# Latent attention: value products in three parts, and three PSUM banks in one rotation for turned pieces, key and query pieces and sums

## The reference

```python
def one(args):
    q_blk, i = args
    s = jnp.einsum('bhqd,bhkd->bhqk', q_blk, k).astype(jnp.float32) * scale
    s = jnp.where(kpos[None, :] <= qpos[:, None], s, neg)
    p = jax.nn.softmax(s, axis=-1).astype(v.dtype)
    return jnp.einsum('bhqk,bhkd->bhqd', p, v)
```

## Time and profile before

| What | us |
|---|---|
| median of 3 runs | 1940.0 |
| the three runs | 1933.75, 1940.00, 1941.69 |
| the profiled execution | 1935.15 |
| its span on the core | 1933.4 |
| TensorE busy | 1832.9 (95%) |
| VectorE busy | 952.6 (49%) |
| ScalarE busy | 667.7 (35%) |
| GpSimd busy | 951.8 (49%) |

### The profile page before, as it was taken

One profiled execution on the slowest core, in us unless ns is written; L12 is line 12 of the kernel. 1 busy time (PEld: TensorE's weight loads), 2 busy tenths in 40 slices (PEclk: granted clock), 3 DMA queues, 4 the chain that ended last, 5 costly groups with the idle time before them and its releaser, 6 DMA issues.

```text
span 1933.4 us, 25385 instructions
## 1 busy us (share of the span) xinstructions
PE 1832.9 (95%) x8924; PEld 1521.7 (79%) x8924; DVE 952.6 (49%) x1420; ACT 667.7 (35%) x1161; POOL 951.8 (49%) x519
## 2 busy tenths in 40 slices
PE   7999999999997888899999989889999999699998
PEld 7788888888876777778878878678888888588887
DVE  5445444000017556675245444577777777622212
ACT  7322223121014555531133222544444444422212
POOL 6733333445654776224533232677777777533230
PEclk9999999999998899999999999899999999899999
DMA  6511101453314885054222133233333333554312
GB/s 259 196 33 44 33 33 55 149 178 120 98 55 149 319 317 217 23 205 144 98 77 66 55 118 112 69 122 122 123 123 121 122 122 112 188 178 130 100 54 87
DMA packets 72667, 237.95 MB, mean 123 GB/s; under 512 B 6800, under 2 KB 17168, under 8 KB 69264
## 3 DMA queue, kind: packets, MB, share of 16 engines
q1 hardware_dynamic: 48720, 159.31, 25.0%
q10 hardware_dynamic: 23872, 77.60, 10.8%
HBM read 172.93 MB, written 63.96 MB: 123 GB/s over the span
## 4 chain that ended last, share of the span: by engine, by line
PE 64%; issue 12%; POOL 12%; DVE 6%; ACT 4%; DMA 1%; POOLq 0%; SPq 0%; ACTq 0%; DVEq 0%
PE ps L554 18%; PE ps L559 18%; PE ps L560 18%; POOL wl L483 8%; PE ps L901 3%; POOL zB L490 2%; PE ps L880 1%; ACT prow L1516 1%; PE ps L1201 1%; PE ps L1203 1%; PE ps L1202 1%; DVE p1l L1890 1%; DMA raw<-in_slabs 1%; DVE kbl L1890 0%; ACT oT L1214 0%
## 5 line engine op out<-in xcount | busy, mean ns | idle before, releaser
L451 POOL TENSOR_SCALAR wh<-raw 128x1024 fp32r<-128x1024 f32 x76 | 211.7, 2786 | 551.5 <-PE ps L554 507.9
L554 PE MATMUL ps<-uh,wh 128*128 128x512 f32 (+1 forms) x576 | 227.8, 395 | 2.4 <-issue 2.4
L560 PE MATMUL ps<-uh,wl 128*128 128x512 f32 (+1 forms) x576 | 224.8, 390 | 0.0
L559 PE MATMUL ps<-ul,wh 128*128 128x512 f32 (+1 forms) x576 | 224.4, 390 | 0.0
L453 POOL TENSOR_TENSOR wl<-raw,wh 128x1024 fp32r<-128x1024 f32 x76 | 183.0, 2408 | 6.4
L483 POOL TENSOR_TENSOR wl<-raw,wh 128x512 fp32r<-128x512 f32 x88 | 139.9, 1609 | 35.3 <-ACT wh L1214 35.3
L530 POOL TENSOR_TENSOR wl<-raw,wh 128x1024 fp32r<-128x1024 f32 x28 | 71.4, 2552 | 141.1 <-ACT wh L1214 141.1
L1893 DVE SCALAR_TENSOR_TENSOR ya<-zA,sm,ya 128x512 f32<-128x512 f32 x88 | 94.1, 1069 | 89.6 <-ACT ya L1748 81.1
L470 POOL TENSOR_TENSOR over_rings<-over_rings 128x512 f32<-128x512 f32 x88 | 112.8, 1282 | 45.9 <-DMA over_rings<-in_slabs 40.6
L1893 DVE SCALAR_TENSOR_TENSOR yb<-zB,sm,yb 128x512 f32<-128x512 f32 x88 | 127.6, 1450 | 14.4 <-ACT yb L1748 8.1
L1214 ACT ACTIVATE wh<-raw 128x512 fp32r<-128x512 f32 (+1 forms) x124 | 90.5, 749 | 114.7 <-PE ps L554 78.4
(11 more groups left out here) (434 smaller groups left out, 4842.3 us busy)
## 6 DMA issues: line engine op xcount, KB each, us to landing
raw<-in_slabs SPq DMA_DIRECT2D x134, 512.0 KB, 3.6
over_rings<-in_slabs SPq DMA_DIRECT2D x22, 1024.0 KB, 7.0
s_s<-over_rings SPq DMA_DIRECT2D x22, 1024.0 KB, 4.8
ssm<-s_s SPq DMA_DIRECT2D x22, 512.0 KB, 3.8
raw<-s_s SPq DMA_DIRECT2D x22, 512.0 KB, 4.8
s_f<-yb ACTq DMA_DIRECT2D x22, 512.0 KB, 2.6
fs<-s_f ACTq DMA_DIRECT2D x22, 512.0 KB, 3.4
a<-in_slabs SPq DMA_DIRECT2D x22, 256.0 KB, 2.6
```

The lines of the kernel that those rows point to most:

```text
L451: pool.tensor_scalar(wh[:, j, :], raw[:, j % RAWS, :], 1.0, None, ALU.mult).then_inc(S["w_hi"], 1)
L554: l = pe.matmul(o, lh, rh, start=start, stop=False)
L559: pe.matmul(o, lh, rl, start=False, stop=False)
L560: return pe.matmul(o, ll, rh, start=False, stop=stop)
```

## The change

Two things, both in the order of work; no instruction is added or left out.

First, `m_pv(g)` is cut into three parts of equal count (`PV_PARTS`): 8 of 24 or 4 of 12 products each. They follow the scores in the steps w mod 4 = 0, 1 and 2 instead of all in the first. The sums' transposes come behind the third part. `m_sum` and `m_out` move from w mod 4 = 1 to w mod 4 = 3. For the last group of all, the three parts stand together as before.

Second, banks 0, 6 and 7 are used in one rotation (`THIRD`) by turned pieces, key and query pieces and sums, in the order in which TensorE makes them (`USES`). Each waits for the use three places back (`BEFORE`, `bank_free`): for `m_ptl` if that was a turned piece, otherwise for `aux_lo`.

```diff
+PV_PARTS = 3
+THIRD = (0, 6, 7)
+USES = [("aux", 0, n) for n in range(4)]
 for _w in range(1, len(UNITS) + 1):
-    if _w < len(UNITS) and _w % NT in AUX_AT and _w // NT + 1 < MH:
-        BANK0.append(("aux", _w // NT + 1, AUX_AT[_w % NT]))
-    if _w % CH == 0:
-        BANK0.append(("sum", _w // CH - 1))
-USE_OF = {e: n for n, e in enumerate(BANK0)}
+    USES += [("turn", _q) for _q in range(PIECE0[_w - 1], PIECE0[_w])]
+    if (_w - 1) % NT in AUX_AT and (_w - 1) // NT + 1 < MH:
+        USES.append(("aux", (_w - 1) // NT + 1, AUX_AT[(_w - 1) % NT]))
+    if _w - 1 > CH and (_w - 1) % CH == PV_PARTS - 1 or _w == len(UNITS):
+        USES.append(("sum", len(UNITS) // CH - 1 if _w == len(UNITS) else (_w - 1) // CH - 1))
+BANK_OF = {e: THIRD[n % 3] for n, e in enumerate(USES)}
+BEFORE = {e: USES[n - 3] for n, e in enumerate(USES) if n >= 3}
+USE_OF = {e: n for n, e in enumerate(e for e in USES if e[0] != "turn")}
...
+            def bank_free(e):
+                if e not in BEFORE:
+                    if BANK_OF[e] == 0:
+                        pe.wait_ge(d_free[0], USE0["vrow"] + NT // 2)
+                    else:
+                        pe.wait_ge(S["k_lo"], 4)
+                elif BEFORE[e][0] == "turn":
+                    pe.wait_ge(S["m_ptl"], BEFORE[e][1] + 1)
+                else:
+                    pe.wait_ge(S["aux_lo"], USE_OF[BEFORE[e]] + 1)
...
-                    at_least(pe, S["m_ptl"], q - 1)
+                    bank_free(("turn", q))
...
-            def m_pv(g):
+            def m_pv(g, part):
...
+                each = [(0, 0), (0, 1)] + [(c, n) for c in range(1, CH * (b + 1)) for n in range(3)] + [(0, 2)]
+                size = len(each) // PV_PARTS
+                for k in range(size * part, size * (part + 1)):
...
+                if part < PV_PARTS - 1:
+                    return
+                l.then_inc(S["m_pv"], 1)
                 pe.wait_ge(S["m_ri"], g + 1)
-                pe.wait_ge(S["aux_lo"], USE_OF["sum", g])
+                bank_free(("sum", g))
...
-                if w and w % CH == 0:
-                    m_pv(w // CH - 1)
-            m_pv(2 * MH - 1)
+                if w >= CH and w % CH < PV_PARTS:
+                    m_pv(w // CH - 1, w % CH)
+            for part in range(PV_PARTS):
+                m_pv(2 * MH - 1, part)
...
-                if w > CH and w % CH == 1:
+                if w > CH and w % CH == PV_PARTS:
                     m_sum(w // CH - 1)
...
-                if w > CH and w % CH == 1:
+                if w > CH and w % CH == PV_PARTS:
                     m_out(w // CH - 1)
```

More of the change, by code:

```diff
@@ L845, in aux @@
                     for j in range(CH):
[L846 removed]
+                        l = pe.transpose(ps[0:QK, a, j * P:(j + 1) * P], qrow[:, CH * b + j, h * QK:(h + 1) * QK],
                                          ident)
@@ L887, in m_pv @@
                 h, b = divmod(g, 2)
[L888 to L893, removed]
+                if part == 0:
+                    pe.wait_ge(S["m_ptl"], PIECE0[CH * (g + 1)])
+                    if g == 0:
+                        for c in range(2):
+                            pe.wait_ge(d_free[c], USE0["vrow"] + NT // 2)
+                    else:
+                        pe.wait_ge(S["aux_lo"], USE_OF["sum", g - 1] + 1)
@@ L894, in m_pv @@
                 ph, pl = (p1h, p1l) if b else (p0h, p0l)
                 v = slice(h // 2 * P, (h // 2 + 1) * P)
-                def one(c, n, start=False, stop=False):
+                each = [(0, 0), (0, 1)] + [(c, n) for c in range(1, CH * (b + 1)) for n in range(3)] + [(0, 2)]
+                size = len(each) // PV_PARTS
+                for k in range(size * part, size * (part + 1)):
+                    c, n = each[k]
                     qs = slice(max(0, c - CH * b) * P, H2)
                     vv, pp = ((vrh, ph), (vrh, pl), (vrl, ph))[n]
-                    return pe.matmul(ps[:, 1, qs], vv[:, c, v], pp[:, c, qs], start=start, stop=stop,
-                                     skip_group_check=True)
@@ L903, in m_pv @@
[L903 to L908, removed]
+                    l = pe.matmul(ps[:, 1, qs], vv[:, c, v], pp[:, c, qs], start=k == 0, stop=k == len(each) - 1,
+                                  skip_group_check=True)
+                if part < PV_PARTS - 1:
+                    return
+                l.then_inc(S["m_pv"], 1)
@@ L1486, in aux_hi @@
                 act.wait_ge(S["aux_t"], USE_OF["aux", h, n] + 1)
-                b = n % 2
+                b, a = n % 2, BANK_OF["aux", h, n]
                 if n < 2:
-                    copy(kbh[0:NOPE, h % 2, half(b)], ps[0:NOPE, 0, :]).then_inc(S["aux_hi"], 1)
+                    copy(kbh[0:NOPE, h % 2, half(b)], ps[0:NOPE, a, :]).then_inc(S["aux_hi"], 1)
                 else:
-                    copy(mqh[0:QK, b, :], ps[0:QK, 0, :]).then_inc(S["aux_hi"], 1)
+                    copy(mqh[0:QK, b, :], ps[0:QK, a, :]).then_inc(S["aux_hi"], 1)
             def m_sum(g):
@@ L1497, in m_sum @@
                 act.wait_ge(S["aux_t"], USE_OF["sum", g] + 1)
-                copy(oT[r, h // 2, half(b)], ps[r, 0, :]).then_inc(S["aux_hi"], 1)
+                copy(oT[r, h // 2, half(b)], ps[r, BANK_OF["sum", g], :]).then_inc(S["aux_hi"], 1)
             def o_hi(fb, b):
@@ L1527, in m_pth @@
                     copy((p1h if g % 2 else p0h)[:, c0:c1, i % CH * P:(i % CH + 1) * P],
-                         ps[:, 6 + q % 2, 0:(c1 - c0) * P].rearrange("p (a n) -> p a n", n=P)).then_inc(
+                         ps[:, BANK_OF["turn", q], 0:(c1 - c0) * P].rearrange("p (a n) -> p a n", n=P)).then_inc(
                         S["m_pth"], 1)
@@ L2189, in aux_lo @@
                 dve.wait_ge(S["aux_hi"], USE_OF["aux", h, n] + 1)
-                b = n % 2
+                b, a = n % 2, BANK_OF["aux", h, n]
                 r = slice(0, NOPE) if n < 2 else slice(0, QK)
                 if n < 2:
-                    lo(kbl[r, h % 2, half(b)], ps[r, 0, :], kbh[r, h % 2, half(b)]).then_inc(S["aux_lo"], 1)
+                    lo(kbl[r, h % 2, half(b)], ps[r, a, :], kbh[r, h % 2, half(b)]).then_inc(S["aux_lo"], 1)
                 else:
-                    lo(mql[r, b, :], ps[r, 0, :], mqh[r, b, :]).then_inc(S["aux_lo"], 1)
+                    lo(mql[r, b, :], ps[r, a, :], mqh[r, b, :]).then_inc(S["aux_lo"], 1)
             def o_lo(fb, b):
@@ L2216, in m_ptl @@
                     lo((p1l if g % 2 else p0l)[at],
-                       ps[:, 6 + q % 2, 0:(c1 - c0) * P].rearrange("p (a n) -> p a n", n=P),
+                       ps[:, BANK_OF["turn", q], 0:(c1 - c0) * P].rearrange("p (a n) -> p a n", n=P),
                        (p1h if g % 2 else p0h)[at]).then_inc(S["m_ptl"], 1)
```

14 lines of the change are left out of this document (5 added, 9 removed).

## The result

| | median us | lowest to highest | runs |
|---|---|---|---|
| before | 1939.88 | 1933.75 to 1941.69 | 4 |
| changed | 1915.36 | 1914.90 to 1916.99 | 4 |

The ratio is 0.9882 (95% interval 0.9865 to 0.9898), 24.5 us less. In a second set of runs the changed kernel took 1912.78 us (1912.09 to 1917.53, 6 runs) against 1938.83 (11 runs), a ratio of 0.9870 (0.9849 to 0.9892).

The account below looks back on a forecast made before the run. TensorE leads but idles about 13%, waiting on round trips through ScalarE and VectorE while its filler work sits elsewhere. Gains 16.5 + 4.4 + 1.5 + 2.4 − 0.5 = 24.3 us, from median 1940.0 to 1916, range 1906 to 1930.

Parts of the forecast that it names:

- r0, r1, r2: A head's first three tile steps, each timed turn to turn: TensorE's work sets them, 9.00 us, a gain of 1.13.
- r3: A head's fourth tile step: the second key piece's wait goes, 2.37 us instead of 2.72, a gain of 0.35.
- r4 and r5: A head's fifth and sixth tile steps: a VectorE and ScalarE chain sets them, 6.53 us, a gain of 1.41.
- r6 and r7: A head's last two tile steps: shared banks make them 2.68 and 2.31 us, a loss of 0.21.
- The new wait behind the query piece: In a head's last tile, the turn's second piece waits for the query piece's bank, about 0.75 us.
- Six heads: The stretch from 651.54 to 805.46 us: each head 22.9 us instead of 25.65, a gain of 16.5 us.
- The first pieces: Head 0's four key and query pieces in three banks: first turn 4.4 us earlier, bounds 2.3 and 4.8.
- Head 0 up to r5: Head 0's fifth tile loses the short products' second and third parts and the sums: a gain of 1.5 us.
- the upper end of the gain: Gain between 18 and 30 us, the upper end if the first steps keep the full clock; timetable's chance 0.70.
- The end: Last head, without key and query pieces, gains 2.4 us; unsplit last products and a longer seventh tile cost 0.5.
- the round trips: Rival, chance 0.20: waits between engines return in a head's later steps, period 24.6 us, time 1928 us.
- The price of the shared rotation: Rival, chance 0.03: turned pieces behind key or query pieces wait 2.3 us each, 9.2 a head, time 1974 us.

Follow-up runs that it names:

- the swap on VectorE: Changed kernel with VectorE's maximum put ahead of the low part of the query piece in the head's fifth tile; 1913.08 us, ratio 0.9866.
- the old start: Changed kernel with only head 0's four key and query pieces again one after another through bank 0; 1919.13 us, ratio 0.9898.
- the experiments with other cuts: Changed kernel with its products in two parts instead of three, 1918.37 us, and in four parts, 1922.37 us.

## Why the prediction was right

The forecast was 1916, the measured median 1915.36. That it is so near is partly luck, since the repeated changed kernel had a median of 1912.78. By its steps, in the first profile of the changed kernel:

- *r0, r1, r2*, 9.00 us forecast, 9.07 measured. TensorE's own work sets all three, without a wait in front of any.
- *r3*, 2.37 forecast, 2.32 measured. The key piece's wait of 0.19 is gone, and the copy of the sums ahead of the turned piece on ScalarE costs nothing.
- *r4 and r5*, 6.53 forecast, 6.46 measured (6.60 in the heads with even numbers), and the swap on VectorE confirmed the chain that was said to set it. This was the part of the sum with the most steps in it. VectorE's two maxima in the head shown:

```profile
716.02 1.21 DVE L2220 TENSOR_REDUCE aneg<-ps 128x1 f32<-128x1024 f32 x1
...
719.59 1.08 DVE L2220 TENSOR_REDUCE aneg<-ps 128x1 f32<-128x896 f32 x1
```

  The first starts 0.63 us behind r4's turn (forecast 0.69), and from it to r6's turn at 721.85 it is 5.83 (forecast 5.84).
- *r6 and r7*, 2.68 and 2.31 forecast, 2.73 and 2.18 measured. The new wait behind the query piece is where it was put. The second piece starts 1.03 us behind the first (724.58 to 725.61), for which I had 1.10 (four blocks in 0.36, then the wait of 0.74). That its row reads 0.42 of idle time and not 0.74 is a matter of the view: a turn's last product still counts as busy while nothing new can start. The forecast for the row had forgotten this.
- *Six heads*, 16.5 us forecast, 153.78 − 136.86 = 16.9 measured.
- *The first pieces*, 4.4 us forecast, 5.26 measured. The first scores come 4.27 earlier (7.84 less 3.57 behind the first key piece), as worked out. But the turn doesn't hang on them. It hangs on ScalarE, which copies the fourth piece (until 634.15 before, 633.93 now), loads a table for 1.28 us and only then makes the first exponential. Before, and now:

```profile
634.17 1.28 ACT L1516 ACT_TABLE_LOAD   x1
...
633.95 1.28 ACT L1530 ACT_TABLE_LOAD   x1
```

  The fourth piece starts 7.10 us behind the first before (632.44 − 625.34) and 2.29 now (632.66 − 630.37), 4.81 less. That is the forecast's upper bound of 4.8, which was the right path. The other 0.45 is the clock: the fourth piece's four transposes take 1.09 us at the lower level (before) and 0.64 at the full one (now), and its copy starts that much sooner behind it. The third piece pays the same: in the profile with the parts alone, where the clock was still full at the third piece, the first turn came 10.30 us behind the first piece and not 10.75.
- *Head 0 up to r5*, 1.5 us forecast, 15.45 − 14.77 = 0.7 in this profile, where the clock was low, and 15.45 − 11.87 = 3.6 in the repeated one, where it was not. Neither is the work alone. Where the clock was low over the same tiles as before, in the profile with the old start, it is 15.45 − 13.90 = 1.5, as forecast. In this profile the low stretch ended later, and r3 took 3.30 us instead of 2.31. The forecast had the clock only as the upper end of the gain; it is worth 2.9 us between the two profiles of one kernel.
- *The end*, 2.4 − 0.5 = 1.9 forecast, 39.96 − 37.85 = 2.1 measured (805.32 to 845.28 before, 787.49 to 825.34 now).

The waits of TensorE for `prow` were forecast at about 6 us and are 2.9, for the same reason as the row of `mql`; `p1l`, forecast at under 4, is gone. ScalarE's wait of 4.61 for the sums, which should have gone, is 2.03: the sums moved behind r2's work, and ScalarE has nothing to do until they are there. The sum of the parts is 25.0 us in this profile and 27.6 in the repeated one, against 24.3. That the medians differ by 24.5 and 26.1 fits both. In this profile the start's 0.9 too little and head 0's 0.8 too much cancel, which is luck.

Two readings in the prediction are off, without weight in the sum. It says that every step but r4 is entered late; by its own rows r1, r3 and r5 are not. And r3's own terms, 0.09 and 2.25, make 2.34 and not 2.37.

Of the rivals, the round trips did not come back: a head never was above 22.93 us. With three banks in rotation and 3.5% idle time the granted clock over six heads was 1.00, as the second row of the first fence shows; if the rotation did anything to the clock, it was at the start and the other way. So the trace doesn't bear out, for this kernel, what the Trainium skill says on cycling through PSUM banks, that it can make the clock swing between its levels (page "TensorE: Matmul & The Clock Gate", section "A second HAM failure mode: psum-queue depth-cycling"). The price of the shared rotation, which I had at 9.2 us a head at worst, showed itself in the experiments with other cuts instead: 0.7 to 0.8 us for each place where a piece meets the sums.

One thing in the forecast is worth correcting. Inside the heads it booked the rotation only as a price, 0.21 us a head, and all of the gain to the parts. The runs show that the parts alone are worth nothing within 2 us and the rotation alone 8.9, nearly all of it at the start. Two thirds of the gain belong to neither alone: they come only with both.

## What to carry to other kernels

When work is moved into an engine's idle steps, its result moves too: look up what the result's buffer is shared with at the new place, and price that wait by a measured trip before counting the gain. Removing a wait for a buffer that ends just ahead of the next wait in the same queue is worth only the distance between the two: here 14.6 us of bank waits became 4.6, and both kinds of wait together stayed at 23.8 where they had been 23.5. And how finely work is spread matters less than where its last part ends: three parts beat two by 0.9 us a head and four by 1.3.

## What the runs showed of the hardware

The granted clock can fall in the middle of the attention, not only at its start. In the profile with only head 0's pieces in three banks it is 0.50, the lower level, in r0 of head 2 and 1.00 a little later (columns as in the first fence):

```profile
684.50:687.50 3.00, 3.00 (x10) 2.67 (x9) 1.53 (x4) 1.05 (x3) 2.76 (x4) 0.50 0.99 284
688.00:691.00 3.00, 3.00 (x18) 2.63 (x17) 0.00 (x0) 0.00 (x0) 1.28 (x2) 1.00 0.97 389
```

Ahead of it lie the late turns of r6, r7 and r0 of that schedule, with TensorE idle for 0.82, 0.67 and 0.65 us before them. It made that head 27.18 us long instead of 25.6. It is the only fall between head 1 and the end of the attention in eleven profiles. That it is in a profile with the old order, and in none of the seven with both parts and rotation, is suggestive and no more than that.

The runs of the kernel before spread over 12 us (1933 to 1945), and the stages ahead of the attention alone over 8 us in eleven profiles of the same code. What varies there is open.
